# Hybrid mLSTM and Hyena backbone on one core: long filters made in the first mixer's output projection; their spectra, the addition of expert results and the row norm in one stage

## The chip, the core and the metric

The kernel runs on one core of a Trainium2 chip. TensorE (PE, with its weight loads as PEld), VectorE (DVE), ScalarE (ACT), GpSimd (POOL) and SyncE (SP, which here only issues transfers) run their own instruction streams and wait for each other by semaphores. The metric is the device time of one execution in microseconds; lower is better.

## What is computed

Two trunk layers over 512 latent tokens of width 1024, with 256 context tokens: an mLSTM mixer, then a Hyena mixer, each followed by a routed expert FFN (32 experts, top 2 in one of 4 groups). All in float32. The part that matters here:

```python
def hyena_filters(L, w1, b1, freq, w2, b2, w3, decay):
    ...
    z = jnp.sin(fr * (feat @ w1.astype(f32) + b1.astype(f32)))
    z = jnp.sin(fr * (z @ w2.astype(f32) + b2.astype(f32)))
    z = z @ w3.astype(f32)
    filt = z * jnp.exp(-tau[:, None] * decay.astype(f32)[None, :])
    return filt * lax.rsqrt(jnp.sum(filt * filt, axis=0, keepdims=True) + EPS)

def fft_long_conv(u, filt, bias):
    ...
    spec = jnp.fft.rfft(uf, n=n, axis=1) * jnp.fft.rfft(filt, n=n, axis=0)[None]
    y = jnp.fft.irfft(spec, n=n, axis=1)[:, L // 2:L // 2 + L]

# reference(), per layer i:
        ul = to_scan_order(rmsnorm(hl, norm1_g[i]) * (1.0 + sc1) + sh1, col_major)
        # layer 0: yl = mlstm_mixer(ul, ...)    layer 1: yl = hyena_mixer(ul, ...)
        hl = hl + g1 * from_scan_order(yl, col_major)
        vl = rmsnorm(hl, norm2_g[i]) * (1.0 + sc2) + sh2
        hl = hl + g2 * moe_ffn(vl.reshape(-1, D), *mo).reshape(B, S, D)
    return rmsnorm(hl, final_g)
```

The filters (512 positions by 2 x 1024 columns) depend on weights alone, not on the tokens. Each column is divided by its norm, and the kernel adds the filter's bias at the centre position.

## The kernel before

The program is a row of stages. Each is a block in which every engine has its own list of instructions in written order; a stage ends with a barrier of all engines and the clearing of its semaphores (`retire`). Nothing of a stage starts before the stage ahead has ended, so order inside a stage is set by the code, and overlap between stages does not exist. The residual stream `hl` (128 partitions x 4 row tiles x 1024) stays on chip.

1. Modulation and input projection (to about 300 us of the trace).
2. The mLSTM heads (block at L1596 to L1942, to 741 us). For each of 4 heads TensorE projects 2 q results, 4 k results (two 512 and two 256 columns wide) and 6 v results (`project`), multiplies the values of the head before (`values`), forms 6 score results, transposes the head before back (`back`) and sums denominators. Results of the projections and scores go round four PSUM banks; `begin(n)` waits until result n - 4 has been copied out (`freed`). ScalarE copies v (L1696), scales the conv output (L1692, which from head 2 on waits for `s_y`, VectorE's gating of two heads before), copies the numerators (L1684) and takes exponentials (L1703). VectorE copies q (L1783) and k (L1788), and then normalises, multiplies scores, finishes the head before, takes reciprocals (L1812) and scales `PW`.
3. Output projection (L1944): TensorE runs over 4 heads, 4 row tiles and 2 column halves with 4 accumulating matmuls each into 8 banks (L1963; each f32 matmul is 2 instructions in the trace, so 128 are 256). `residual` (L186, L187) adds the banks times the gate to `hl` after the last head. SP loads the weights of heads 1 to 3.
4. Routing and experts of layer 0 (`expert_ffn`), then `combine`: SP loads the sorted-back results (`yg`, four transfers of 1 MB), VectorE adds two weighted rows per token (L229).
5. `filters` (L740 to L886): 13 small loads; the two sine layers of the small network on 64 partitions (L787, L789, L850 to L855, L818); 16 filter tiles of 128 positions x 512 columns (L797), each multiplied by its envelope (L823, L861), squared on ScalarE (L834) and summed over positions by matmuls that give one column of 128 (L782) per quarter. The norms so lie as 128 x 16 numbers; `rsqrt` (L99 to L104: 2 integer operations and 12 float ones, each waiting for the one before) inverts them, four matmuls spread them over partitions (L804), VectorE scales the tiles (L873 to L876). Then 6 spectra (L732, L735; 3 groups of frequencies for each of 2 filters): TensorE fills four banks, ScalarE copies two of them (L839, L840), VectorE writes 4 sums and differences to `Fs` (L883 to L886). The spectra alternate between banks 0 to 3 and 4 to 7.
6. `hyena_mix` (L902): squares of the rows on ScalarE (L959), `rsqrt`, scaled rows `xh` (L999), transposes (L1078) with ScalarE writing `uh` (L963), then the projections (L1156), convolutions, forward and inverse transforms, output.
7. Routing, experts and `combine` of layer 1, and a last stage with the final row norm (L2006 to L2017) and the stores.

## Time and profile before

| | us |
|---|---|
| runs | 2569.49, 2572.08, 2572.23 (median 2572.08) |
| the profiled execution | 2573.89, span 2572.2, mean granted TensorE clock 0.906 |
| busy in the span | TensorE 2143.8, VectorE 804.0, ScalarE 275.0, GpSimd 286.7 |
| heads of the mLSTM, from 360 to 741 | 381 |
| output projection, from 741 to 856 | 115 |
| routing of layer 0, from 856 to 922 | 66 |
| experts of layer 0, from 922 to 1456 | 534 |
| adding the results, from 1456 to 1473 | 17 |
| filters and spectra, from 1473 to 1612 | 139 |
| row norm to the first projection, from 1612 to 1631 | 19 |
| last two stages, from 2539 | 33 |

The profile takes one execution; times in it are microseconds from the span's start. A timeline row gives the start, the length, the engine, the line in the kernel, the output tile and its inputs, how many instructions are merged in the row, and in brackets how long the engine had been idle and what released it. Rows of one engine overlap a little, since the next instruction starts while the last one drains. PEclk is the share of full clock granted to TensorE: 1.0 is 2.4 GHz, 0.5 is 1.2 GHz.

### The profile page before, as it was taken

How to read it: one execution, taken by the hardware profiler on the slowest of the kernel's cores; microseconds unless marked ns; L12 is line 12 of the kernel's file. 1: busy time of each engine (PE TensorE's matmuls, PEld its weight loads, DVE VectorE, ACT ScalarE, POOL GpSimd, SP SyncE). 2: the span in 40 equal slices, each digit the busy share in tenths (PEclk: the TensorE clock that was granted, in tenths of full speed). 3: DMA queues.
4: the chain of work that ended last, by engine and by line, in shares of the span. 5: the costliest groups of instructions: out<-in, count | busy, mean ns of one | idle time of the engine just before them, and what ended most of it. 6: DMA issues, size and time to landing. Idle time of an engine off the chain costs nothing. (4 is left out here: it accounts for less than half of the span.)

```text
span 2572.2 us, 20183 instructions
## 1 busy us (share of the span) xinstructions
PE 2143.8 (83%) x7640; PEld 978.2 (38%) x7640; DVE 804.0 (31%) x1407; ACT 275.0 (11%) x503; POOL 286.7 (11%) x545
## 2 busy tenths in 40 slices
PE   5998999999789669888887489799996698888972
PEld 2554444444334423333333143344454233333320
DVE  3775204325520531111111224255745311111113
ACT  2111212201100100000000031211101000000000
POOL 0000000000000312121221000000003121212210
PEclk9999999999889679999999758899996799999996
DMA  8897412220020669999999320112017699999992
GB/s 325 325 362 253 160 50 98 92 88 17 0 98 0 261 243 407 407 407 408 407 404 407 150 66 1 62 63 69 17 66 273 233 407 407 407 408 407 405 377 112
DMA packets 179008, 588.31 MB, mean 229 GB/s; under 512 B 22408, under 2 KB 40064, under 8 KB 171529
## 3 DMA queue, kind: packets, MB, share of 16 engines
q1 hardware_dynamic: 153470, 548.51, 54.9%
q10 hardware_dynamic: 13260, 21.40, 2.4%
q0 software_dynamic: 12160, 16.83, 1.9%
q8 instruction: 75, 1.23, 0.2%
q14 instruction: 43, 0.35, 0.0%
HBM read 571.61 MB, written 38.12 MB: 237 GB/s over the span
## 5 line engine op out<-in xcount | busy, mean ns | idle before, releaser
L603 PE MATMUL bank<-w,xT0e 128*64 128x512 f32 x1184 | 283.0, 633 | 59.2 <-DMA w<-in_moe_w 57.9
L603 PE MATMUL bank<-w,xT1e 128*64 128x512 f32 x1152 | 278.0, 638 | 58.6 <-DMA w<-in_moe_w 57.3
L603 PEld LDWEIGHTS bank<-w,xT0e 128*64 128x64 f32 x1184 | 104.5, 146 | 233.4 <-issue 231.5
L603 PEld LDWEIGHTS bank<-w,xT1e 128*64 128x64 f32 x1152 | 101.6, 147 | 230.9 <-issue 228.9
L1156 PE MATMUL bank<-uhi,wnh 128*128 128x512 f32 x384 | 168.4, 593 | 0.9 <-ACT uhi L963 0.9
L623 PE MATMUL bank<-w,hT0e 128*64 128x512 f32 x592 | 135.2, 597 | 8.3 <-issue 7.3
L623 PE MATMUL bank<-w,hT1e 128*64 128x512 f32 x576 | 131.5, 597 | 7.7 <-issue 6.6
L1505 PE MATMUL bank<-uT,wo 128*128 128x512 f32 x256 | 132.0, 597 | 0.5 <-DVE uT L1393 0.5
L691 DVE COPY hT0e<-bank 128x256 f32<-128x256 f32 x37 | 15.7, 425 | 311.4 <-PE bank L611 311.4
L691 DVE COPY hT1e<-bank 128x256 f32<-128x256 f32 x36 | 15.3, 425 | 312.1 <-PE bank L611 312.1
L1842 PE MATMUL bank<-uT,wo 128*128 128x512 f32 x256 | 110.7, 593 | 0.0
L1156 PEld LDWEIGHTS bank<-uhi,wnh 128*128 128x128 f32 x384 | 71.8, 190 | 86.9 <-issue 85.8
L1416 DVE SCALAR_TENSOR_TENSOR acc<-adab,cv,acc 128x2048 f32<-128x2048 f32 x35 | 82.3, 2350 | 16.9 <-DMA adab<-in_ada_w 16.1
L1654 POOL TENSOR_SCALAR_AFFINE_SELECT PW<-PW 128x128 f32<-128x128 f32 x32 | 10.9, 344 | 654.4 <-ACT PW L1703 653.1
L1893 PE MATMUL bank<-vw,xmh 128*128 128x512 f32 x192 | 83.0, 592 | 0.0
L1963 PE MATMUL bank<-ow,yT 128*128 128x512 f32 x192 | 82.6, 592 | 0.0
L1506 PE MATMUL bank<-uT,wo 128*128 128x256 f32 x256 | 76.1, 379 | 0.0
L623 PEld LDWEIGHTS bank<-w,hT0e 128*64 128x64 f32 x592 | 46.7, 136 | 73.0 <-issue 73.0
L623 PEld LDWEIGHTS bank<-w,hT1e 128*64 128x64 f32 x576 | 45.5, 136 | 70.6 <-issue 70.6
L1506 PEld LDWEIGHTS bank<-uT,wo 128*128 128x128 f32 x256 | 48.6, 190 | 61.2 <-issue 61.2
L1842 PEld LDWEIGHTS bank<-uT,wo 128*128 128x128 f32 x256 | 48.4, 190 | 61.6 <-issue 61.6
L696 DVE TENSOR_TENSOR yb0e<-bank,g2h 128x512 f32<-128x512 f32 x37 | 25.6, 692 | 122.4 <-PE bank L623 115.8
(580 smaller groups left out, 2544.9 us busy)
## 6 DMA issues: line engine op xcount, KB each, us to landing
w<-in_moe_w SPq DMA_DIRECT2D x65, 4096.0 KB, 29.1
w<-in_moe_w SPq DMA_DIRECT2D x65, 2048.0 KB, 23.9
adab<-in_ada_w SPq DMA_DIRECT2D x24, 2048.0 KB, 11.4
wnh<-in_h_in_w SPq DMA_DIRECT2D x12, 1024.0 KB, 5.2
wo<-in_m_in_w SPq DMA_DIRECT2D x4, 2048.0 KB, 10.8
wo<-in_m_in_w ACTq DMA_DIRECT2D x4, 2048.0 KB, 17.2
yg<-d_y SPq DMA_DIRECT2D x8, 1024.0 KB, 6.9
d_xm<-xmb ACTq DMA_DIRECT2D x16, 385.5 KB, 5.9
```

The lines of the kernel that those rows point to most:

```text
L603: ins = t_.matmul(b[n * C:(n + 1) * C, :].rearrange("c (g f) -> c g f", g=2), xT[:, k, half * C:(half + 1) * C], w13s[:, u, kk, n], start= ...
L623: ins = t_.matmul(b_y[m * C:(m + 1) * C, :], hT[:, k, half * C:(half + 1) * C], w2[:, u, kk, m * 512:(m + 1) * 512], start=(kk == 0), stop ...
L691: v.tensor_copy(hT[:].rearrange("p k n -> p (k n)"), b_h[:, 0:2 * P]).then_inc(S["hT"], 1)
L696: v.tensor_tensor(yb[:], b_y[:], g2h[:], ALU.mult).then_inc(S["ya"], 1)
L1156: ins = t_.matmul(bank[i % 2][:], wn[:, q % 2, k, f * P:(f + 1) * P], uh[:, k, :], start=(k == 0), stop=(k == KD - 1))
L1416: ins = v.scalar_tensor_tensor(out=a_, in0=w, scalar=s, in1=a_, op0=ALU.mult, op1=ALU.add)
L1505: t_.matmul(bank[2 * (i % 2)][:], w, uT[:, k, CTX:NTOK], start=(k == 0), stop=(k == KD - 1))
L1506: ins = t_.matmul(bank[2 * (i % 2) + 1][:, 0:CTX], w, uT[:, k, 0:CTX], start=(k == 0), stop=(k == KD - 1))
L1654: g.affine_select(out=dg, in_=dg, compare_op=ALU.is_ge, fill=0.0, base=0, pattern=[[step, P]], channel_multiplier=-step).then_inc(s_msk, 1)
L1842: ins = t_.matmul(bank[n % 4][:], wo[h % 2][:, k, f * P:(f + 1) * P], uT[:, k, CTX:NTOK], start=(k == 0), stop=(k == KD - 1))
L1893: ins = t_.matmul(b, xmh[:, f, c0:c0 + P], vw[:, f, :], start=(f == 0), stop=(f == FT - 1))
L1963: ins = nc.tensor.matmul(bank[2 * t + n][:], yT[:, i * FT + f, t * P:(t + 1) * P], ow[i][:, f, n * 512:(n + 1) * 512], start=(i == 0 and f ...
```

## The change

Four things change.

First, in the heads, the six copies of q and k per head go from VectorE's list to ScalarE's, between the scaling of the conv output and the copies of v.

Second, `filters` disappears as a stage. What makes the filters moves into the stage of the output projection. The projection is split into column halves: half 0 over all heads into banks 0 to 3, then half 1 into the same banks. Banks 4 and 5 take filter tiles, 6 and 7 the column sums. From the sixth group of half 0 on, one tile and one column sum follow each group; the last five tiles follow behind half 0. The sums are now formed with a full matrix of ones over 512 columns, so each partition holds them, and `rsqrt` works on 128 x 512 elements, four times. Finished filters are stored to memory (`d_fl`, 4 x 1 MB).

Third, `hyena_mix` loads the filters back, and in one stage forms the six spectra, adds the expert results (`combine` is gone as a stage) and takes the row norm. The filters and results use tiles that are free at that time.

Fourth, the last stage adds the expert results of layer 1, with the squares of a row tile following its addition.

```diff
-        def combine(l, wts):
-            with stage() as c:
...
+        def load_results(sp, l, yg, s_yg):
+            for t in range(TL):
+                sp.dma_start(yg[t], d_y[l].rearrange("(t p k) d -> t p k d", p=P, k=2)[t]).then_inc(s_yg[t], 16)
+
+        def add_results(dve, own, t, yg, s_yg):
+            dve.wait_ge(s_yg[t], 16)
+            for k in range(2):
+                own(nc.vector.scalar_tensor_tensor(out=hl[:, t, :], in0=yg[t][:, k, :], scalar=wts[:, k, t:t + 1], in1=hl[:, t, :], op0=ALU.mult, op1=ALU.add))
...
-        def filters(Fs, wn, s_wn):
...
@@ hyena_mix, SP
+                    sp.dma_start(dft[:], I["dft"].rearrange("(t p) f -> p t f", p=P)).then_inc(S["dft"], 16)
+                    for o in range(2):
+                        for h in range(2):
+                            sp.dma_start(flo[o][:, :, h * 512:(h + 1) * 512], d_fl[2 * o + h]).then_inc(s_flo[o], 16)
+                        if o == 0:
+                            load_results(sp, 0, yg, s_yg)
+                    for q in range(2):
+                        load_slab(sp, wn, s_wn, q)
@@ hyena_mix, ScalarE
+                    for i in range(6):
+                        odd_parts(i)
+                        if i in (1, 2):
+                            for t in range(2 * i - 2, 2 * i):
+                                act.wait_ge(S["hl"], t + 1)
+                                at_least(act, S["sq"], t)
+                                a.activation(junk, hl[:, t, :], ACT.Square, accum_out=ss[:, t:t + 1]).then_inc(S["sq"], 1)
@@ hyena_mix, VectorE
+                    for i in range(6):
+                        filter_spectra(i)
+                        if i < 2:
+                            for t in range(2 * i, 2 * i + 2):
+                                add_results(dve, own, t, yg, s_yg)
+                                v.memset(r1[:, t:t + 1], 0.0).then_inc(S["hl"], 1)
+                        if i == 3:
+                            dve.wait_ge(S["sq"], TL)
...
+                            rsqrt(v, own, r1[:], ss[:], r2[:])
+                            for t in range(TL):
+                                v.tensor_scalar(xh[:, t, :], hl[:, t, :], ss[:, t:t + 1], None, ALU.mult).then_inc(S["xh"], 1)
@@ hyena_mix, TensorE
+                    pe.wait_ge(S["dft"], 16)
+                    for i in range(6):
+                        o, g = i // 3, i % 3
+                        if g == 0:
+                            pe.wait_ge(s_flo[o], 32)
+                        at_least(pe, S["fs"], i - 1)
+                        spectrum(t_, dft, lambda pk, h: flo[o][:, pk, h * 512:(h + 1) * 512], lo if i % 2 == 0 else hi, g).then_inc(S["sps"], 1)
                     pe.wait_ge(S["xh"], TL)
+                    pe.wait_ge(S["fs"], 5)
@@ output projection, SP (after ten small loads of the filters)
                 for i in range(1, HEADS):
                     sp.dma_start(ow[i], out_rows(i)).then_inc(s_ow[i], 16)
+                for n in range(4):
+                    sp.wait_ge(s_fin, n + 1)
+                    sp.dma_start(d_fl[n], fl[n // 2][:, :, (n % 2) * 512:(n % 2 + 1) * 512]).then_inc(s_flst, 16)
+                sp.wait_ge(s_flst, 64)
@@ output projection, VectorE
+                for i in range(NT4):
+                    dve.wait_ge(s_zps, 3 + i)
+                    dve.wait_ge(s_E, i + 1)
+                    v.tensor_tensor(tile(i), bank[4 + i % 2][:], E[:, i % 2, :], ALU.mult).then_inc(s_g, 1)
+                    if i % TL == 1 and i > TL:
+                        square_sum(i // TL - 1)
                 dve.wait_ge(s_x4, 32)
+                add_projection(0)
+                square_sum(3)
+                for n in range(4):
+                    dve.wait_ge(s_smv, n + 1)
+                    r = fsum[:, n, :]
+                    rsqrt(v, own, kx[:], r, ft[:])
...
+                    own(v.tensor_tensor(centre, centre, r, ALU.mult))
+                    v.tensor_tensor(centre[0:1, :], centre[0:1, :], brow[:, cs], ALU.add)
+                    for t in (0, 2, 3):
+                        x = tile(n * TL + t)
+                        ins = v.tensor_tensor(x, x, r, ALU.mult)
+                    ins.then_inc(s_fin, 1)
+                add_projection(1)
@@ output projection, TensorE (FIRST = 5)
+                pe.wait_ge(s_fld, 16 * 6)
+                t_.matmul(bank[4][0:HFH, :], fw1[:], ft[0:HEMB, :], start=True, stop=True).then_inc(s_zps, 1)
+                for g, (i, t) in enumerate(groups):
+                    project(0, i, t)
+                    if g == 2:
+                        pe.wait_ge(s_zz, 1)
+                        t_.matmul(bank[4][0:HFH, :], fw2[:], z[0][:], start=True, stop=True).then_inc(s_zps, 1)
+                    if g >= FIRST:
+                        filter_tile(g - FIRST)
+                    if g >= FIRST + 1:
+                        square_column(g - FIRST - 1)
+                done = len(groups) - FIRST
+                for i in range(done, NT4):
+                    filter_tile(i)
+                    square_column(i - 1)
+                square_column(NT4 - 1)
+                for i, t in groups:
+                    project(1, i, t)
@@ last stage, VectorE
+                for t in range(TL):
+                    add_results(dve, own, t, yg, s_yg)
+                    v.memset(r1[:, t:t + 1], 0.0).then_inc(s_hlf, 1)
```

The functions named in it do this: `add_projection(n)` takes the four banks of a half, each a product with the gate and an addition to `hl`; `square_sum(n)` copies a sum out of its bank with the epsilon added; `filter_tile` and `square_column` are one matmul each, the first waiting for VectorE's multiplication two tiles back, the second for ScalarE's square of its tile; `odd_parts` and `filter_spectra` are the copies and sums that `filters` had.

The order of the instructions shows it at three places. VectorE, heads: behind head 0's scaling of `PW` stand, before, the copies of head 1's q and k.

```order
L1819 TENSOR_TENSOR PW<-PW,uT 128x128
L1819 TENSOR_TENSOR PW<-PW,uT 128x512
L1822 TENSOR_TENSOR PW<-PW 128x128
L1783 COPY qT<-bank 128x512 x2
L1788 TENSOR_SCALAR kT<-bank 128x512
L1788 TENSOR_SCALAR kT<-bank 128x256
L1788 TENSOR_SCALAR kT<-bank 128x512
L1788 TENSOR_SCALAR kT<-bank 128x256
L1758 BN_STATS st<-hh 128x6 x4
```

After, the statistics of head 0's values follow at once; `L1655` is the line of the statistics, `L1707` and `L1710` those of the scaling.

```order
L1707 TENSOR_TENSOR PW<-PW,uT 128x128
L1707 TENSOR_TENSOR PW<-PW,uT 128x512
L1710 TENSOR_TENSOR PW<-PW 128x128
L1655 BN_STATS st<-hh 128x6 x4
L1658 BN_AGGR mv<-st 128x2 x3
L1659 BN_AGGR mv<-st 128x2
L1660 TENSOR_SCALAR var<-mv 128x4
L99 TENSOR_SCALAR r<-var 128x4
```

The copies have left VectorE's row. On ScalarE they now stand behind the four scalings (written to a part of `wo`):

```order
L1580 ACTIVATE wo<-xch,colT 128x512 x4
L1584 ACTIVATE qT<-bank 128x512 x2
L1589 ACTIVATE kT<-bank 128x512
L1589 ACTIVATE kT<-bank 128x256
L1589 ACTIVATE kT<-bank 128x512
L1589 ACTIVATE kT<-bank 128x256
L1593 ACTIVATE wo<-bank 128x512 x6
```

There they come ahead of the six v copies. TensorE, output projection (`uT` holds the weights of head 0, `ow` the others, `fw` and `z` belong to the small network), before:

```order
L1523 UNCONDITIONAL_BRANCH
L1955 UNCONDITIONAL_BRANCH
L1963 MATMUL bank<-uT,yT 128x512 x32
L1963 MATMUL bank<-ow,yT 128x512 x96
L1944 UNCONDITIONAL_BRANCH
```

After:

```order
L1977 MATMUL bank<-ft,fw 64x512
L1955 MATMUL bank<-uT,yT 128x512 x12
L1982 MATMUL bank<-z,fw 64x512
L1955 MATMUL bank<-uT,yT 128x512 x4
L1955 MATMUL bank<-ow,yT 128x512 x8
L1966 MATMUL bank<-fw,z 128x512
L1955 MATMUL bank<-ow,yT 128x512 x4
L1966 MATMUL bank<-fw,z 128x512
L1973 MATMUL bank<-sqf,onesmat 128x512
L1955 MATMUL bank<-ow,yT 128x512 x4
L1966 MATMUL bank<-fw,z 128x512
L1973 MATMUL bank<-sqf,onesmat 128x512
```

The projection that was one run of 128 matmuls is now cut after every four by a tile and a column sum. TensorE, between the experts of layer 0 and the Hyena projections, before (the last tile, the sums, the spread norms, the spectra, and in the next stage the transposes):

```order
L797 MATMUL bank<-w3f,z1f 128x512
L782 MATMUL bank<-onesmat,sqf 128x1 x8
L804 MATMUL bank<-dgf,onesmat 128x512 x4
L732 MATMUL bank<-flf,dftf 128x512 x16
L735 MATMUL bank<-flf,dftf 64x512 x16
L732 MATMUL bank<-flf,dftf 128x512 x16
L735 MATMUL bank<-flf,dftf 64x512 x16
L740 UNCONDITIONAL_BRANCH
L1071 UNCONDITIONAL_BRANCH
L1078 MATMUL bank<-ident,Pri 128x128 x32
L1156 MATMUL bank<-uhi,wnh 128x512 x16
```

After (`vti` and `uhi` hold the filters that were loaded back):

```order
L493 UNCONDITIONAL_BRANCH
L950 UNCONDITIONAL_BRANCH
L720 MATMUL bank<-vti,dfti 128x512 x16
L723 MATMUL bank<-vti,dfti 64x512 x16
L720 MATMUL bank<-uhi,dfti 128x512 x16
L723 MATMUL bank<-uhi,dfti 64x512 x16
L965 MATMUL bank<-ident,Pri 128x128 x32
L1044 MATMUL bank<-uhi,wnh 128x512 x16
```

The spectra are now the first work behind the experts, and no barrier stands between them and the transposes.

## Rows read from the trace of the kernel before

**Rows 1.** Stages: stretch, length, busy PE PEld DVE ACT POOL, PEclk, DMA share, GB/s
```profile
741.00:856.00 115.00, 112.45 (x256) 49.50 (x256) 11.06 (x16) 0.00 (x0) 0.00 (x0) 0.98 0.14 55
1473.00:1564.00 91.00, 71.00 (x172) 39.64 (x172) 29.43 (x69) 22.55 (x35) 0.00 (x0) 0.51 0.17 51
```

**Rows 2.** TensorE's timeline, heads 0 to 3: start, us, line, work, [idle before <-releaser]
```profile
430.75 5.33 PE L1884 MATMUL bank<-xch,kw 128*128 128x512 f32 x16
441.10 7.69 PE L1884 MATMUL bank<-xch,kw 128*128 128x512 f32 x16 [5.03 <-DVE qT L1783]
...
528.52 8.35 PE L1884 MATMUL bank<-xch,kw 128*128 128x512 f32 x16 [5.03 <-DVE qT L1783]
...
557.31 20.76 PE L1903 MATMUL bank<-wo,PW 128*128 128x512 f32 x48
...
616.60 6.99 PE L1884 MATMUL bank<-xch,kw 128*128 128x512 f32 x16 [5.03 <-DVE qT L1783]
...
702.71 23.74 PE L1903 MATMUL bank<-wo,PW 128*128 128x512 f32 x48 [16.46 <-DVE PW L1822]
```

**Rows 3.** Groups by line, ScalarE in the heads: xcount | busy us, mean ns | idle
```profile
L1684 ACT ACTIVATE hh<-bank 128x512 f32<-128x512 f32 x16 | 9.6, 598 | 107.8 <-PE bank L1903 107.8
```

**Rows 4.** VectorE's timeline after head 0, ScalarE's timeline before head 2
```profile
440.36 1.28 DVE L1783 COPY qT<-bank 128x512 f32<-128x512 f32 x2
...
508.54 2.56 ACT L1692 ACTIVATE wo<-xch,colT 128x512 f32<-128x512 f32 x4 [11.83 <-DVE yT L1777]
```

**Rows 5.** Timeline of the output projection, TensorE, and the next stage's first transfer
```profile
741.35 30.05 PE L1963 MATMUL bank<-uT,yT 128*128 128x512 f32 x64 [4.48 <-PEq L121]
771.23 82.56 PE L1963 MATMUL bank<-ow,yT 128*128 128x512 f32 x192
...
856.56 0.34 SPq L259 DMA_DIRECT2D vt0r<-in_norm_g  x1
```

**Rows 6.** Timeline, start of the filter stage, all engines
```profile
1473.36 0.38 SPq L759 DMA_DIRECT2D ftf<-in_feat_t  x1
...
1478.33 1.96 PE L787 MATMUL bank<-ftf,w1f 33*64 33x512 f32 x2 [36.43 <-DMA pcf<-in_h_f_freq]
...
1481.71 0.42 DVE L852 TENSOR_SCALAR kxf<-kxf 64x512 f32<-64x512 f32 x1
...
1484.05 0.63 ACT L818 ACTIVATE z0f<-z0f 64x512 f32<-64x512 f32 x1 [46.86 <-DVE z0f L855]
```

**Rows 7.** VectorE's timeline, first block of the filter scaling
```profile
1558.89 0.68 DVE L874 TENSOR_TENSOR flf<-flf,browf 1x512 f32<-1x512 f32 x1
1559.50 1.86 DVE L876 TENSOR_TENSOR flf<-flf,bank 128x512 f32<-128x512 f32 x3
```

**Rows 8.** TensorE's timeline, two of the sixteen filter tiles
```profile
1500.77 2.07 PE L797 MATMUL bank<-w3f,z1f 64*128 64x512 f32 x2
...
1504.56 2.07 PE L797 MATMUL bank<-w3f,z1f 64*128 64x512 f32 x2
```

**Rows 9.** Timeline, expert results added and row norm; first projection of the Hyena mixer
```profile
1456.32 2.39 SPq L220 DMA_DIRECT2D yg<-d_y  x4
...
1620.40 2.74 DVE L999 TENSOR_SCALAR Pri<-hl,ssi 128x1024 f32<-128x1024 f32 x4
...
1630.95 14.00 PE L1156 MATMUL bank<-uhi,wnh 128*128 128x512 f32 x32 [0.87 <-ACT uhi L963]
```

**Rows 10.** Transfers of the expert results, both layers, by tile
```profile
DMA to landing us min/median/max: 4.7/6.9/8.8
```

**Rows 11.** TensorE's timeline, spectra 3 and 4 of six
```profile
1587.17 14.00 PE L732 MATMUL bank<-flf,dftf 128*128 128x512 f32 x32
```

**Rows 12.** Timeline of the last two stages: VectorE, ScalarE, VectorE
```profile
2543.95 10.53 DVE L229 SCALAR_TENSOR_TENSOR hl<-yg,wts,hl 128x1024 f32<-128x1024 f32 x8 [19.51 <-DMA yg<-d_y]
...
2555.83 1.06 ACT L2006 ACTIVATE junkf<-hl 128x1024 f32<-128x1024 f32 x1 [41.86 <-PEq L121]
...
2560.56 0.17 DVE L2013 TENSOR_SCALAR ssz<-ssz 128x4 f32<-128x4 f32 x1 [6.08 <-ACT junkf L2006]
```

326 lines of the change are left out of this document (136 added, 190 removed).

## The prediction

> **What bounds the kernel now.** I read the view of stages first, then TensorE's timeline through each stage that the diff touches, then, where TensorE stood idle, the timeline of the engine named behind the arrow. Four places come out.
>
> In the four heads of the first mixer TensorE runs nearly without a break, except that heads 1 to 3 each stop for 5.03 us in the middle of the k projection, until VectorE has copied the first q result out of its bank [rows 2]. VectorE does that copy at 440.36, behind the reciprocal and scaling of the head before [rows 4]. After each stop the 16 matmul instructions take 7.69, 8.35 and 6.99 us, where the 16 of the same shape ahead of the stop took 5.33 [rows 2].
>
> In the output projection TensorE is the bound: 112.45 of 115 us busy at a granted clock of 0.98, the 2.4 GHz level [rows 1, 5].
>
> From 1473 to 1564 us the filters are made by a chain of three engines. TensorE counts 71 of 91 us as busy, but its clock is 0.51, the 1.2 GHz level [rows 1], and its tiles come 3.79 us apart (1500.77 to 1504.56) [rows 8].
>
> Between the first transfer of the expert results at 1456.32 and the Hyena mixer's first projection at 1630.95 lie 174.6 us [rows 9]: adding the results, the filters, their spectra, and the row norm, one after another.
>
> **Step 1, q and k copied out by ScalarE.** Removed: 6 copies per head in VectorE's queue. Added: 6 on ScalarE, each about 0.60 us, the price of its other copies from a bank [rows 3]. In ScalarE's queue they stand behind the four scalings of the head's conv output. Before head 2 those start at 508.54, held by VectorE's gating of head 0, and end at 511.1 [rows 4]. The stop of that head begins at 528.52 - 5.03 = 523.5 [rows 2], behind two q results and two k results (3 x 3.44 us, and 1.7 for the one of 256 columns: 12.0), so the first q result starts at about 511.5 and is complete at 514.9: ScalarE is free in time, by 3.8 us. A bank is then emptied 0.6 us after it is full, and is wanted again only three results later: the stop goes. Gain 3 x 5.03 = 15.1 us, and the slow matmuls behind it, 7.69 + 8.35 + 6.99 - 3 x 5.33 = 7.0 us: **-22.1**. The later waits of a head hang on TensorE's own value products and move along with them. Bounds: -15.1, if the clock still falls for another reason, and -22.1.
>
> **Step 2, the filters in the output projection's stage.** Before, from TensorE's first matmul at 741.35 to the next stage's first transfer at 856.56, this took 115.2 us [rows 5]. I count after from the stage's start, S.
> - TensorE now waits first for six small loads. In the filter stage these cost 1478.33 - 1473.36 = 5.0 us [rows 6].
> - Up to the second half's first matmul it has half of the projection, 128 instructions, 4 of the small network, 32 of tiles and 32 of column sums: 196, at 82.56 / 192 = 0.43 us each [rows 5] 84.3 us.
> - The start at 1.2 GHz: 48 instructions took 23.74 us after a wait of 16.46, and 20.76 without [rows 2]: 3.0 us. For the last five tiles, which no projection covers, I add 1.5 us (estimate; a tile and a column sum fill 1.72 us of TensorE, and VectorE's 0.68 and ScalarE's 0.63 follow each other beside it).
> So the second half starts at S + 93.8. The small network's first sine ends 6.4 us after its matmul began (1478.33 to 1484.68) [rows 6], less than the three projection groups of 3.4 us set in front of the next one: no wait. The 6 MB of output weights are now queued behind 1.6 MB more; the first is wanted only after four groups, 23 us in, so I cost that at nothing; without that cover it would be a few us.
> - From there TensorE needs 128 x 0.43 = 55.0 us, but VectorE more. It starts about 1.6 us ahead, on four bank additions of two operations each (8 x 0.72 = 5.8) and one sum (0.7). Then come four blocks: an inverse square root over 128 x 512 elements, which was over 128 x 16. Its two integer operations at 0.45 (0.42 for a 512-wide operation with constants [rows 6], and the step to the next) and twelve at 0.72 (0.68 [rows 7] and the step) give 9.5; the scaling is 0.72 + 0.61 + 1.86 = 3.1 [rows 7]. Four blocks are 50.6 us. The filters are complete at +55.5, and four more bank additions end at +61.3. The last 1 MB store, of the size of the result loads, takes 4.7 to 6.9 us [rows 10] and lands at about +61.5. The end of a stage costs 0.7, half of the 1.35 us from 2554.48 to 2555.83, where two are closed [rows 12].
> The stage lasts 93.8 + 61.5 + 0.7 = 156 us and a little for a store that takes longer; I take 157: **+41.8**. VectorE, not TensorE, ends it. Bounds: +35 if the wide operations run at the 0.62 pitch of the scaling and TensorE ends the stage (55.0 + 1.4 for the last addition), +52 if each tile's wait costs TensorE 0.6 us more. The routing stage behind it begins with TensorE idle for 7 us instead of 3: **+1** (0 to 2).
>
> **Step 3, spectra, expert results and norm in one stage.** Instead of 174.6 us I find: 0.7 for one stage end more in front; 9.5 until the transform matrix and the first filters (2.9 MB) have landed, since four result transfers of 1 MB land 4.7 to 8.8 us after issue [rows 10] and the four together took about 11 (range 7 to 14); the first spectrum, 7.0 (half of 14.00 [rows 11]) and 3.0 for the clock; five more at 7.03, 35.2; then 7.8 from the transposes to the first projection (1623.14 to 1630.95 [rows 9]). VectorE fits under it: six spectra at 2.4 us, eight result additions at 1.32 (10.53 for eight [rows 12]), 3 us of small operations and 2.74 us of row scaling [rows 9] make 31 us, in 42. In its order, the scaled rows are ready 30.6 us after the first spectrum's end and the fifth spectrum's sums at 33, and TensorE comes to the transposes at 35.2. No bank is waited for: spectrum 4 needs the sums of spectrum 2, ready at 20, and starts at 21. The clock, now at 2.4 GHz through the transposes, may give 1 us. Sum 63.2: **-111.4**. Bounds -116 and -105.
>
> **Step 4, the last stage.** The squares of a row tile now run under the next tile's addition: 2555.83 to 2560.56 are 4.7 us, of which the last square, 1.3, stays; and 0.7 of a stage end goes: **-4.1** [rows 12].
>
> **The sum:** -22.1 + 41.8 + 1 - 111.4 - 4.1 = -94.8. The profiled execution took 2573.9 us (span 2572.2, and 1.7 around it), and would take 2479.1. The median of the runs, 2572.1, gives **2477**. The two expert stages only move in time: their weight transfers start with the routing stage, as before.
>
> **Rivals.**
> A: ScalarE comes no earlier to the q results than VectorE did, because its scalings wait for VectorE's gating. Then step 1 brings nothing: 2477 + 22 = 2499. Against it stand the 3.8 us of slack, and that the gating itself moves forward with the head.
> B: the filter tiles keep their own chain inside the projection. If each of 16 costs 3.79 us as in [rows 8] instead of 1.72, that is 16 x 2.07 = 33 us more: 2510. For it: the order of engines is the same. Against it: 11 of the 16 have four projection matmuls (3.4 us) between them, longer than VectorE's and ScalarE's shares together.
> C, the other side: the merged stage runs at 1.2 GHz. In the filter stage just these tiles and sums ran at a clock of 0.51 although TensorE was busy for 78% of it [rows 1]. TensorE would then need 5 + 196 x 0.86 + 1.5 + 128 x 0.86 = 285 us and 2 for the end, 130 more than forecast: 2607, slower than before. It decides from 95 / 0.43 = 221 of the 324 instructions at the low level. Against it: 256 of them are the same projection matmuls that ran at 0.98 [rows 1], and the waits in between are under 1 us.
> The Trainium skill speaks for C: "TensorE: Matmul & The Clock Gate", section "A second HAM failure mode: psum-queue depth-cycling", says that short idles between groups of matmuls, as banks are cycled, can make the clock swing between its levels. By that rule the time would be C's or a part of it; in the heads of this trace banks are cycled all the time, and only the 5 us stops are followed by slow matmuls [rows 2], so the trace does not agree with it for waits this short.
>
> **How the numbers follow.** Forecast 0.77, with a range of its own of 2464 to 2492 (steps 2 and 3 by their bounds, not both at their ends). A 0.10, B 0.09, C 0.04. The range reaches to A and leaves out B, C and the forecast's own ends: 2464 to 2501. A change under 0.2% can't be told from none here. Forecast, A and B are faster: 0.95; C is slower: 0.04; 0.01 for a mixture that cancels out.
>
> **What would show it.** Right: no wait of TensorE on q copies; the next stage after the projection 157 us after its start, with VectorE last; the projection at a clock above 0.95; 63 us from the end of the first expert stage to the Hyena mixer's first projection. Wrong: a falling clock in the projection, square root operations over 0.72 us, spectra that wait for filters from memory beyond 14 us, or transposes that wait for VectorE.

## The result and the profile after

The changed kernel takes 2450.07 us (median of 4 runs, 2449.15 to 2453.90), the kernel before 2570.86 beside it (4 runs, 2569.49 to 2572.23): a ratio of 0.9533, with a 95% interval of 0.9516 to 0.9550. That is faster, as forecast, but by 120.8 us instead of 95, and 2450 lies outside the range of 2464 to 2501. The profiled execution has a span of 2452.2 us, 120.0 less than that of before.

The first thing to do with such a miss is to cut both traces at the same points and subtract. SyncE's first transfer of each stage is a good mark, since nothing of a stage starts before it. These are the marks after, from SyncE's timeline (start, length, line, what is loaded):

```profile
717.38 0.32 SPq L1857 DMA_DIRECT2D ft<-in_feat_t  x1
...
879.24 0.35 SPq L247 DMA_DIRECT2D vt0r<-in_norm_g  x1
...
1470.61 0.38 SPq L777 DMA_DIRECT2D dfti<-in_dft  x1
...
1849.16 0.34 SPq L247 DMA_DIRECT2D vt1r<-in_norm_g  x1
...
2423.83 2.07 SPq L212 DMA_DIRECT2D ygf<-d_y  x4
```

The same marks before are 741.30, 856.56 [rows 5], 1456.32 [rows 9] and these two:

```profile
1947.88 0.34 SPq L259 DMA_DIRECT2D vt1r<-in_norm_g  x1
...
2539.21 1.91 SPq L220 DMA_DIRECT2D yg<-d_y  x4
```

The Hyena mixer's first projection stands at 1630.95 [rows 9] before and at 1532.14 after.

| stretch | before | after | difference | forecast |
|---|---|---|---|---|
| start to output projection | 741.3 | 717.4 | -23.9 | -22.1 (Step 1) |
| output projection stage | 115.3 | 161.9 | +46.6 | +41.8 (Step 2) |
| routing and experts of layer 0 | 599.8 | 591.4 | -8.4 | +1 (Step 2) |
| first result transfer to first projection | 174.6 | 61.5 | -113.1 | -111.4 (Step 3) |
| rest of the Hyena mixer | 316.9 | 317.0 | +0.1 | 0 |
| routing and experts of layer 1 | 591.3 | 574.7 | -16.6 | 0 |
| last stage | 33.0 | 28.4 | -4.6 | -4.1 (Step 4) |

The four steps together miss by 1 us, and that is partly luck: Step 2 came out 4.8 us dearer, and Steps 1, 3 and 4 together 4.0 us better. What the forecast missed lies in the routing and expert stages, where the diff changes no instruction's work and only moves one small tile: 25 us less, where it had said +1. TensorE there waits for weights. In the view of waits (in us: total, times, longest), TensorE's waits for the weight transfers, both layers together, stood at 115.1 us before:

```profile
PE bank L603 <- DMA w<-in_moe_w: 115.1, 38, 4.7
```

and after they are 19 us shorter:

```profile
PE bank L591 <- DMA w<-in_moe_w: 95.8, 35, 4.3
```

The windows view shows more. Of two stretches of 200 us inside the expert stages it gives the busy time of PE, PEld, DVE, ACT, POOL, then the clock, the DMA share and the GB/s. Before:

```profile
1100.00:1300.00 200.00, 166.01 (x738) 64.59 (x736) 24.92 (x56) 10.79 (x28) 40.11 (x85) 0.95 1.03 407
2130.00:2330.00 200.00, 174.30 (x774) 67.90 (x774) 24.91 (x56) 10.78 (x28) 39.53 (x85) 0.94 1.03 407
```

After:

```profile
1100.00:1300.00 200.00, 174.72 (x792) 69.33 (x790) 26.68 (x60) 11.55 (x30) 42.60 (x90) 0.96 1.03 419
2130.00:2330.00 200.00, 173.75 (x790) 68.75 (x788) 26.69 (x60) 11.55 (x30) 40.19 (x86) 0.97 1.02 419
```

The DMA engines are busy throughout in both (shares of 1.02 and 1.03), but move 419 GB/s instead of 407. So the question is not when these transfers start, but why the same transfers run 3% faster.

### The profile page after: what moved, and what is told of

Its sections match the earlier page's. It is cut to its first block and busy times, and to the rows that moved or that the text cites. A ratio compares the mean times of both kernels' runs of the same rounds, so it can differ in the third digit from the quotient of the medians.

```text
span 2452.2 us, 19965 instructions
## 1 busy us (share of the span) xinstructions
PE 2091.9 (85%) x7536; PEld 944.2 (39%) x7536; DVE 825.7 (34%) x1420; ACT 289.5 (12%) x529; POOL 286.7 (12%) x545
## 5 line engine op out<-in xcount | busy, mean ns | idle before, releaser
L591 PE MATMUL bank<-w,xT1e 128*64 128x512 f32 x1152 | 271.9, 626 | 49.8 <-DMA w<-in_moe_w 48.3
L1730 PEld LDWEIGHTS bank<-uT,wo 128*128 128x128 f32 x256 | 48.4, 190 | 61.5 <-issue 61.5
L662 ACT ACTIVATE sg0e<-bank 128x256 f32<-128x256 f32 x37 | 14.3, 385 | 452.3 <-PE bank L591 452.3
## 6 DMA issues: line engine op xcount, KB each, us to landing
w<-in_moe_w SPq DMA_DIRECT2D x65, 4096.0 KB, 28.4
```

The lines of the kernel that those rows point to most:

```text
L591: ins = t_.matmul(b[n * C:(n + 1) * C, :].rearrange("c (g f) -> c g f", g=2), xT[:, k, half * C:(half + 1) * C], w13s[:, u, kk, n], start= ...
L662: a.activation(sg[:], b_gu[u][:, 0:DE // 2], ACT.Silu).then_inc(S["sg"], 1)
L1730: ins = t_.matmul(bank[n % 4][:], wo[h % 2][:, k, f * P:(f + 1) * P], uT[:, k, CTX:NTOK], start=(k == 0), stop=(k == KD - 1))
```

## Experiments: why the expert weights arrive faster

One tile that the diff moves offers a reason.

```diff
+        wts = sbt(top, "wts", [P, 2, TL])
...
-                wts = sbt(c, f"wts{l}", [P, 2, TL])
```

The small tile `wts` (32 bytes in each partition) moves from the expert stage, where it stood behind the weight tiles, to the top of on-chip memory, and pushes all that comes behind it up by 32 bytes. Read from the addresses that the program is built with, the weight tile `w13` (two thirds of the weight bytes; rows of 4096 bytes) goes from byte 37088 of each partition to 37120, and `w2` from 135392 to 135424. The first pair are multiples of 32 only, the second of 256. The diff also declares a new tensor in main memory, `d_fl`, which moves `d_y`, where results are scattered. I tested both.

**Undoing the shift in the changed kernel.** Two pads in the expert stage alone; the rest of the change stays.

```diff
+                pa = sbt(c, f"pa{l}", [P, 8])
                 w13 = sbt(c, f"w13_{l}", [P, NB, KD, 2 * DE])
...
                 g2h = sbt(c, f"g2h{l}", [P, D // 2])
+                pb = sbt(c, f"pb{l}", [P, 8])
```

> The changed kernel, computing the same, with 32 bytes a partition put ahead of the expert weight tiles in the expert stages and 32 more behind them. The change had moved a 32-byte tile (wts) to the top of the on-chip memory, so that the weight tiles w13 and w2 start at byte 37120 of each partition, a multiple of 64, where they started at 37088, a multiple of 32 only. This kernel puts them at 37152, a multiple of 32 only, and leaves all else of the change. Theory P (place of the weight tiles): the two expert stages lose what they won, about 8 + 17 = 25 us, so 2475 us, and the transfers in them run at 406 to 408 GB/s instead of 418 to 420. Theory M (place in main memory: the new tensor d_fl moves d_y, to which results are scattered): nothing changes, 2450 us and 419 GB/s. Theory O (another part of the change, or the chip's own spread): nothing changes either.

Measured: 2477.56 us, ratio 0.9645 (0.9629 to 0.9661). Routing and experts take 602.5 and 587.8 us instead of 591.4 and 574.7, and the gain of these stages is gone. This is the changed kernel with its weight tiles at bad places, as they were before, and so the kernel that the prediction priced: 2477.6 us against the forecast 2477, a sum whose terms partly cancel. The two stretches of 200 us:

```profile
1100.00:1300.00 200.00, 172.77 (x774) 67.74 (x770) 25.36 (x58) 11.26 (x30) 39.66 (x84) 0.95 1.03 407
2130.00:2330.00 200.00, 166.74 (x732) 64.52 (x732) 24.89 (x56) 10.65 (x28) 37.05 (x79) 0.93 1.03 407
```

**The same pads in the kernel before**, with nothing else of the change.

> The kernel before, computing the same, with the same 32 bytes ahead of the expert weight tiles, which puts w13 at 37120, a multiple of 64. Theory P: 25 us faster than the kernel before, about 2547 us, with 418 to 420 GB/s in the expert stages. Theories M and O: no change, 2572 us and 407 GB/s.

Measured: 2546.26 us, ratio 0.9912 (0.9895 to 0.9928), 23 us faster (19 to 27 by the interval); the two stretches are 585.7 and 576.6 us long.

```profile
1100.00:1300.00 200.00, 169.50 (x764) 66.55 (x764) 25.98 (x59) 11.17 (x30) 39.63 (x84) 0.96 1.03 420
2130.00:2330.00 200.00, 176.45 (x794) 69.40 (x792) 25.98 (x59) 11.54 (x30) 42.08 (x88) 0.95 1.03 419
```

**The new tensor in main memory alone**, declared in the kernel before and not used.

```diff
         d_v = [dram(f"d_v{i}", [SEQ, D]) for i in range(2)]
+        d_fl = dram("d_fl", [4, P, TL, 512])
```

> The kernel before, computing the same, with the new tensor d_fl declared in main memory but not used, so that d_y0 and d_y1 lie 4 MB further, as in the changed kernel. Theory M: 25 us faster, about 2547 us, 419 GB/s in the expert stages. Theories P and O: no change, 2572 us, 407 GB/s.

Measured: 2569.84 us, ratio 1.0000 (0.9990 to 1.0009), and 407 GB/s. Theories M and O fall. The place of the tiles in the expert stage carries the 25 us: taken away in the changed kernel, it costs 27.5 us, and given to the kernel before, it brings 23.

**Which places are good.** Two runs with 64 bytes ahead of `w13`, as here, and with 128 (32 elements of 4 bytes instead of 16):

```diff
+                pa = sbt(c, f"pa{l}", [P, 16])
                 w13 = sbt(c, f"w13_{l}", [P, NB, KD, 2 * DE])
```

> The changed kernel, computing the same, with 64 bytes ahead of w13: both weight tiles start at a multiple of 64 that is no multiple of 128 (37184 and 135488), where the changed kernel's were multiples of 128. If a multiple of 64 is what counts: no change, ratio 0.9533, 419 GB/s in the expert stages. If a multiple of 128 counts: as with 32 bytes, 0.9645 and 407 GB/s, or something between.

Measured: 2478.43 us, ratio 0.9637 (0.9621 to 0.9653), 407 GB/s. I had expected a multiple of 64 to be enough. It is not.

> The changed kernel, computing the same, with 128 bytes ahead of w13: w13 at 37248 and w2 at 135552, both odd multiples of 128, where the changed kernel's 37120 and 135424 were multiples of 256. Shifts of 32 and of 64 bytes cost 24 to 28 us each. If a multiple of 128 is what counts: no change, ratio 0.9533, 419 GB/s in the expert stages. If a multiple of 256 counts: 0.964 and 407 GB/s. (37120 is no multiple of 512, so nothing beyond 256 is needed.)

Measured: 2478.16 us, ratio 0.9644 (0.9628 to 0.9660), again 407 GB/s. A multiple of 128 is not enough either. So far three shifts cost the same, and the changed kernel's place might have been good for some reason of its own. The run with 256 bytes tells:

> The changed kernel, computing the same, with 256 bytes ahead of w13: w13 at 37376 and w2 at 135680, both multiples of 256. Shifts of 32, 64 and 128 bytes cost 24 to 28 us each (ratios 0.9637 to 0.9645, 407 GB/s in the expert stages). Theory (a multiple of 256 bytes is what counts): as the changed kernel, ratio 0.953, 419 GB/s. Rival (37120 is good for another reason, such as its distance to other tiles, and any shift spoils it): 0.9640, 407 GB/s.

Measured: 2451.48 us, ratio 0.9532 (0.9517 to 0.9548), stretches of 589.3 and 575.1 us:

```profile
1100.00:1300.00 200.00, 176.14 (x796) 69.73 (x794) 26.68 (x60) 11.52 (x30) 40.71 (x87) 0.96 1.03 419
2130.00:2330.00 200.00, 173.92 (x790) 69.07 (x792) 26.68 (x60) 11.49 (x30) 41.44 (x89) 0.97 1.02 419
```

A multiple of 256 bytes is what counts among the places tried; how far off it the tile lies (32, 64, 128, or 224 as before) makes no difference that these runs can tell. The Trainium skill has a rule that fits: "DMA: Bandwidth & Descriptors", section "How a descriptor splits into AXI transactions", says that the transactions of a transfer start at 256-byte boundaries, so that a piece which doesn't begin at one has its first transaction start at the boundary below, and spends beats of 32 bytes on what lies before its start. That page of the Trainium skill speaks of reading, while the tiles here are written to. As an estimate from the same page of the Trainium skill, if a row of 4096 bytes is one piece of 128 beats, 32 bytes off would add 1 beat (0.8%), 128 bytes 4 (3.1%) and 224 bytes 7 (5.5%). The runs agree with the boundary, but not with a cost by beats: here all of these places cost 2.9% (407 against 419). Why the price is the same at every distance stays open.

**Which tile.** Four runs misplace one tile alone, or both by different amounts. The pad in front of `w2` moves the small tiles behind it too. First `w2` by 32 bytes:

> The changed kernel, computing the same, with 32 bytes between w13 and w2: w13 stays at a multiple of 64 and only w2, a third of the bytes, goes to a multiple of 32 only. Theory P with a cost per byte: a third of the 25 us comes back, 8 us, so 2458 us, with 415 GB/s in the expert stages; the median time to landing of the w2 transfers (24.0 us) grows and not that of w13 alone. If only the first tile's place counted, 2450 us; if any misplaced tile spoiled the whole, 2475 us. Theories M and O: 2450 us.

Measured: 2455.89 us, ratio 0.9560 (0.9544 to 0.9576), 418 GB/s, stretches of 592.4 and 576.9 us. The median time to landing of the `w2` transfers did not grow: 23.4 us, and 24.0 in the changed kernel. Then by 64 bytes:

> The changed kernel, computing the same, with 64 bytes between w13 (stays at 37120) and w2 (135488, an odd multiple of 64). With 32 bytes there the ratio was 0.956, 3 to 7 us over the changed kernel; with 32 ahead of w13 and 64 ahead of w2 it was 0.9634, and with 64 ahead of both 0.9637. If the cost lies with the w13 transfers mostly: a ratio of 0.954 to 0.957 again and 418 GB/s. If it is a cost per byte of whichever tile: 0.957, 415 GB/s. If one misplaced tile of two were enough for the whole at this distance: 0.9635, 407 GB/s.

Measured: 2453.56 us, ratio 0.9545 (0.9529 to 0.9561), 419 and 417 GB/s, stretches of 590.8 and 576.2 us. Then 32 bytes ahead of `w13` and 32 behind it:

> The changed kernel, computing the same, with 32 bytes ahead of w13 and 32 behind it: w13, two thirds of the weight bytes, starts at a multiple of 32 only, w2 at a multiple of 64. Putting both there cost 25 us (ratio to the kernel before 0.9645 instead of 0.9533), w2 alone 3 to 7 us. Theory P with a cost per byte: two thirds of 25 us, 17 us, a ratio of 0.960. Theory P with w13 as the carrier (w2 alone cost less than its third): 18 to 22 us, 0.9605 to 0.962. Had the cost lain only in both being misplaced together: under 5 us, 0.955.

Measured: 2478.38 us, ratio 0.9634 (0.9618 to 0.9650). I had planned it as a run with `w13` alone misplaced, and counted a multiple of 64 as a good place for `w2`. The runs above show that it is none, so this run has both misplaced and says only that the two offsets need not be equal. The run that does separate them:

```diff
+                pa = sbt(c, f"pa{l}", [P, 32])
                 w13 = sbt(c, f"w13_{l}", [P, NB, KD, 2 * DE])
+                pb = sbt(c, f"pb{l}", [P, 32])
```

> The changed kernel, computing the same, with 128 bytes ahead of w13 and 128 behind: w13 at an odd multiple of 128 (37248), w2 at a multiple of 256 (135680). w2 alone misplaced gave ratios of 0.956 and 0.9545 against 0.9533. Theory (w13 carries it): 0.9625 to 0.9645. A cost per byte: 0.960. If both have to be misplaced: 0.953 to 0.955.

Measured: 2464.49 us, ratio 0.9584 (0.9568 to 0.9600), and between the two rates:

```profile
1100.00:1300.00 200.00, 174.67 (x786) 68.61 (x783) 25.99 (x59) 11.54 (x30) 39.77 (x84) 0.95 1.03 414
2130.00:2330.00 200.00, 174.69 (x780) 68.00 (x779) 24.91 (x56) 10.77 (x28) 40.05 (x85) 0.94 1.02 414
```

So `w13` alone costs about 13 us and both together 24 to 29. That meets none of the three expectations for this last run; the nearest is the cost per byte, 0.960, at the edge of the interval. What `w2` alone costs is less sure. By the ratios its two runs lie 3 and 7 us above the changed kernel, but the intervals overlap with that kernel's. The two expert stages together took 1167.0 and 1169.2 us in them, and 1164.4 to 1168.9 in the seven runs made from the changed kernel with both tiles well placed, where single stretches of 200 us show 417 to 420 GB/s. Both tiles misplaced cost more than the two costs added; a transfer into a well placed tile seems to take up part of what a misplaced neighbour in the queue loses. That is a reading, and no run isolates it.

**Is it general?** The big early loads go to places that are no multiples of 256 in both kernels.

```diff
+        pc = sbt(c12, "pc12", [P, 32])
         wo = [sbt(c12, f"wo{i}", [P, KD, DH]) for i in range(2)]
...
+            pd = sbt(c1, "pd", [P, 48])
             adab = [sbt(c1, f"adab{i}", [P, 2, 2048]) for i in range(2)]
```

> The changed kernel, computing the same, with the targets of the big early loads put at multiples of 256 bytes: adab0 and adab1 (from 173504 and 189888 to 173824 and 190208) and wo0 and wo1 (from 94592 and 110976 to 94720 and 111104). Up to 200 us of the trace these loads keep the DMA engines busy nearly throughout (shares of 0.97, 0.77, 1.00 and 0.96 in four stretches of 50 us) but TensorE too. If the rule is general and the early stages hang on the loads: 3 per cent of up to 150 us, 4 to 5 us less, ratio 0.9515. If TensorE's work hides the loads, or if the rule holds for the expert weights alone: no change, 0.9533.

Measured: 2452.15 us, ratio 0.9534 (0.9518 to 0.9550): no change that can be told. The `adab` transfers did land a little earlier. By tile, their time to landing in the changed kernel (minimum, median, maximum) is

```profile
DMA to landing us min/median/max: 7.8/11.3/19.7
```

and in this run

```profile
DMA to landing us min/median/max: 7.6/10.9/19.2
```

The output projection begins at 715.48 here, and between 716.43 and 719.00 in the other runs made from the changed kernel, so up to 1 us may have been won. The place is worth something where a stage hangs on its transfers, as the expert stages do; here TensorE is busy beside them.

## Experiments: the steps of the prediction

**Step 1 alone.** The six copies of q and k move to ScalarE in the kernel before.

```diff
-                if kind == "v":
+                if kind in ("q", "k", "v"):
...
+                    for i in range(QT):
+                        n = NUM["q", h, i]
+                        act.wait_ge(s_pj, n + 1)
+                        a.activation(qT[:, i, :], bank[n % 4][:], ACT.Copy).then_inc(s_evA, 1)
```

> The kernel before, computing the same, with the first part of the change alone: the six copies of q and k of each head by ScalarE. The prediction's Step 1: 22.1 us faster, ratio 0.9914, and TensorE waits for no copy of q in the second to fourth head, head period 80 us. Rival A (ScalarE comes late from head 2 on): 0 to 11 us, ratio over 0.9957. If the first part only helped together with the others, no change, ratio 1.0.

Measured: 2546.69 us, ratio 0.9900 (0.9884 to 0.9917), 25 us faster. TensorE's timeline shows the k projection in one piece, where before it was two with a stop between them [rows 2]:

```profile
429.92 10.49 PE L1884 MATMUL bank<-xch,kw 128*128 128x512 f32 x32
...
509.76 10.49 PE L1884 MATMUL bank<-xch,kw 128*128 128x512 f32 x32
...
589.61 10.49 PE L1884 MATMUL bank<-xch,kw 128*128 128x512 f32 x32
```

Each head now takes 79.8 us.

**Step 2, its start.** TensorE's first projection group goes ahead of its wait for the filter loads.

```diff
-                pe.wait_ge(s_fld, 16 * 6)
-                t_.matmul(bank[4][0:HFH, :], fw1[:], ft[0:HEMB, :], start=True, stop=True).then_inc(s_zps, 1)
                 for g, (i, t) in enumerate(groups):
                     project(0, i, t)
-                    if g == 2:
+                    if g == 0:
+                        pe.wait_ge(s_fld, 16 * 6)
+                        t_.matmul(bank[4][0:HFH, :], fw1[:], ft[0:HEMB, :], start=True, stop=True).then_inc(s_zps, 1)
+                    if g == 3:
```

> The changed kernel, computing the same, with TensorE's list at the start of the output projection in another order: the first group of the projection stands ahead of the small network's first matmul and its wait for the filter loads, and the second matmul one group later. In the changed kernel TensorE stands idle there for 5.0 us, and its clock is at half until 5.6 us later. Theory: the idle time goes, 5 us less, 2445 us, ratio 0.9513, and the second half of the projection starts 94 to 95 us after the stage's start instead of 99.8. Rival: the wait for the copy of z moves behind and gives it back, or the half clock holds as long after the first matmul as now (then about 7 us of the first groups' work still runs at half): 2 to 3 us less. If the end of the stage hung on VectorE's chain from a fixed time, no change.

Measured: 2445.66 us, ratio 0.9509 (0.9493 to 0.9525). The stage takes 156.6 us (718.53 to 875.12) and its second half starts at 813.08, 94.6 us after its start. The wait is gone and nothing took its place.

**Step 2, its layout.** GpSimd adds the squares of a block, 4 column sums replace 16, filter tiles run on into the second half, and VectorE inverts blocks between tiles.

```diff
+            @blk.gpsimd
...
+                        own(nc.gpsimd.tensor_tensor(fsum[:, n % 3, :], fsum[:, n % 3, :], sqf[:, t % 2, :], ALU.add))
...
+                AFTER = {5: [(inverse, 0)], 7: [(scaled, 0)], 10: [(add_projection, 0)], 11: [(inverse, 1)], 13: [(scaled, 1)],
+                         14: [(inverse, 2)], 15: [(scaled, 2), (inverse, 3), (scaled, 3)]}
...
+                    if j in (4, 8, 12, 19):
+                        column_sum(min(j // TL - 1, 3))
```

> The changed kernel, computing the same, with the output projection's stage laid out anew: TensorE starts at once (as in the run before), filter tiles go on one per group into the second half, GpSimd adds the squares of a block so that 4 column sums on TensorE take the place of 16, and VectorE inverts and scales the blocks between the tiles. Theory (the stage is bound by TensorE's list up to the second half and then by VectorE's chain of 62 us, so what counts is TensorE's work and an earlier start of that chain): TensorE's 256 projection instructions at 0.43 us, 110 us, plus 16 tiles and 4 sums at 0.96, 19, plus 5 us for the network and the slow clock, plus 3 us at the end: 137 us for the stage instead of 161.9, so 25 us less, 2425 us, ratio 0.9436. Rival (VectorE falls behind, so that TensorE waits for banks while a block is inverted, or GpSimd's additions slow VectorE): 10 to 18 us less, 0.9465 to 0.9495. Rival (the stage is bound by the VectorE chain however it starts): no more than the 5 us of the run before, 0.9510.

Measured: 2441.80 us, ratio 0.9499 (0.9483 to 0.9514): the stage takes 149.7 us instead of 161.9, not 137. TensorE's timeline names two waits:

```profile
785.66 2.08 PE L1990 MATMUL bank<-fsum,onesmat 128*128 128x512 f32 x2 [4.44 <-POOL fsum L1907]
787.52 4.29 PE L1974 MATMUL bank<-ow,yT 128*128 128x512 f32 x8
...
798.93 5.40 PE L1974 MATMUL bank<-uT,yT 128*128 128x512 f32 x8 [1.38 <-DVE tmp L1927]
```

After each wait its instructions are slower: 5.40 us for 8, where 3.70 is the rule in this stage. The first wait is for GpSimd, and GpSimd's timeline shows an operation of one size at two prices:

```profile
749.05 1.27 POOL L1907 TENSOR_TENSOR fsum<-fsum,sqf 128x512 f32<-128x512 f32 x1 [101.16 <-ACT sqf L1896]
753.80 1.27 POOL L1907 TENSOR_TENSOR fsum<-fsum,sqf 128x512 f32<-128x512 f32 x1 [3.47 <-ACT sqf L1896]
...
780.61 5.00 POOL L1907 TENSOR_TENSOR fsum<-fsum,sqf 128x512 f32<-128x512 f32 x2 [10.53 <-ACT sqf L1896]
...
820.01 2.92 POOL L1907 TENSOR_TENSOR fsum<-fsum,sqf 128x512 f32<-128x512 f32 x1 [11.67 <-ACT sqf L1896]
...
835.12 3.44 POOL L1907 TENSOR_TENSOR fsum<-fsum,sqf 128x512 f32<-128x512 f32 x1 [10.54 <-ACT sqf L1896]
```

An addition took 1.27 us while VectorE was idle, and 2.92 and 3.44 beside VectorE's scaling, which reads two on-chip tiles. GpSimd's spans are rough, but VectorE's own operations beside it went up too, as this one of the scaling, which takes 0.68 otherwise [rows 7]:

```profile
781.03 1.64 DVE L1946 TENSOR_TENSOR wo<-wo,brow 1x512 f32<-1x512 f32 x1
```

**The same, with two orders changed**, so that a sum is asked for later and the bank additions stand ahead of a tile.

```diff
-                AFTER = {5: [(inverse, 0)], 7: [(scaled, 0)], 10: [(add_projection, 0)], 11: [(inverse, 1)], 13: [(scaled, 1)],
+                AFTER = {5: [(inverse, 0)], 7: [(scaled, 0)], 9: [(add_projection, 0)], 11: [(inverse, 1)], 13: [(scaled, 1)],
...
-                    if j in (4, 8, 12, 19):
-                        column_sum(min(j // TL - 1, 3))
+                    if j in (4, 10, 13, 19):
+                        column_sum((4, 10, 13, 19).index(j))
```

> The kernel of the run with the projection stage laid out anew (0.9499), computing the same, with two waits of TensorE taken out by order alone: the second and third column sum stand two groups and one group later, and VectorE adds the first half of the projection ahead of the eleventh filter tile instead of behind it. In that run TensorE waited 4.44 us for a slow addition on GpSimd and 1.38 us for a bank, and ran some 3 us slower behind them. Theory: 5.8 us of waits and about 3 us of slow clock go, 2433 us, ratio 0.9465. Rival (the sums wait at their new places, since GpSimd's additions take 3 to 5 us beside VectorE's): 2 to 4 us, 0.9485.

Measured: 2434.77 us, ratio 0.9467 (0.9452 to 0.9483). The stage takes 140.5 us, and between its first matmul and the next stage TensorE waits for no other engine. This kernel beats the changed one by 0.6% to 0.7%, with intervals that do not overlap, and is the fastest of the study. The gain of 7 us is for both orders together.

**Step 3, the overlap alone.** Results and norm come behind all six spectra, still in one stage.

```diff
                     for i in range(6):
                         filter_spectra(i)
-                        if i < 2:
-                            for t in range(2 * i, 2 * i + 2):
-                                add_results(dve, own, t, yg, s_yg)
...
+                    for t in range(TL):
+                        add_results(dve, own, t, yg, s_yg)
+                        v.memset(r1[:, t:t + 1], 0.0).then_inc(S["hl"], 1)
```

> The changed kernel, computing the same, with the results added and the row norm taken after all six spectra instead of between them, still in one stage. It tells what of Step 3 is overlap. In the changed kernel the transposes start at 1524.97 with no wait for VectorE. Here VectorE's eight additions (1.3 us each), the last square, the inverse root and the four scalings (10.5 + 1.3 + 3.1 + 2.7 us) come behind its last writes of the spectra (3.7 us after the last spectrum): 21 us later, 2471 us, ratio 0.9615. With TensorE's clock at half after the idle time, the transposes take some 3 us more, 2474 us, 0.9627. If the overlap were worth little because the transfers of the results end late, under 10 us.

Measured: 2475.73 us, ratio 0.9630 (0.9614 to 0.9646). By the trace the stretch to the first projection grows from 61.5 to 82.5 us (1471.41 to 1553.95), and TensorE waits where the changed kernel does not:

```profile
1517.79 7.09 PE L723 MATMUL bank<-uhi,dfti 128*64 128x512 f32 x32
1546.15 5.41 PE L962 MATMUL bank<-ident,Pri 128*128 128x128 f32 x24 [21.28 <-DVE Pri L875]
```

So 21 of the 113 us of Step 3 are overlap of the norm and the results. The rest is, by subtraction, the filters, which are no longer made here, and the stage ends.

## Why the prediction was wrong

**The step that failed** is the sentence behind the sum: "The two expert stages only move in time: their weight transfers start with the routing stage, as before." Their start did not change, but their rate did, from 407 to 419 GB/s, since the diff moved their target by 32 bytes onto a multiple of 256. That is 25 us by the two stretches, and 23 to 28 by the runs that move the tiles alone, of the 27 us between forecast and result. The profile of before could not show it as a gain waiting to be had: it shows one rate. What it did show is that these two stretches of some 600 us hang on the weights (115.1 us of TensorE's waits in them), so everything that touches the weight tiles, their place too, had to be looked at. The line that moves `wts` stood in the diff, and I passed over it as one without a cost. With -25 in its place the forecast would have been about 2452.

**Step 1** was right in mechanism and a little small: 23.9 us in the trace, 25 as a change of its own (interval 21 to 30), against 22.1. Of the part not counted, 0.8 us is the last head's numerator, 22.96 us for the instructions that took 23.74 [rows 2], and 0.5 us lies ahead of the second head; 0.5 us more is not traced. Rival A fell: no stop is left.

```profile
430.26 10.49 PE L1772 MATMUL bank<-xch,kw 128*128 128x512 f32 x32
...
510.11 10.49 PE L1772 MATMUL bank<-xch,kw 128*128 128x512 f32 x32
```

**Step 2** had its structure right and one term too small. The second half began 99.8 us after the stage's start, not 93.8:

```profile
722.34 1.96 PE L1977 MATMUL bank<-ft,fw 33*64 33x512 f32 x2 [9.39 <-DMA pc<-in_h_f_freq]
724.23 12.51 PE L1955 MATMUL bank<-uT,yT 128*128 128x512 f32 x24
736.67 1.07 PE L1982 MATMUL bank<-z,fw 64*64 64x512 f32 x2
...
753.91 1.13 PE L1973 MATMUL bank<-sqf,onesmat 128*128 128x512 f32 x2
754.87 3.60 PE L1955 MATMUL bank<-ow,yT 128*128 128x512 f32 x8
758.40 1.12 PE L1966 MATMUL bank<-fw,z 64*128 64x512 f32 x2
759.45 1.12 PE L1973 MATMUL bank<-sqf,onesmat 128*128 128x512 f32 x2
...
813.27 1.12 PE L1966 MATMUL bank<-fw,z 64*128 64x512 f32 x2
814.32 1.12 PE L1973 MATMUL bank<-sqf,onesmat 128*128 128x512 f32 x2
816.23 1.12 PE L1973 MATMUL bank<-sqf,onesmat 128*128 128x512 f32 x2 [0.78 <-ACT sqf L1891]
817.19 8.32 PE L1955 MATMUL bank<-uT,yT 128*128 128x512 f32 x19
```

The start is as forecast: 5.0 us of waiting, then 14.3 us for 26 instructions, 3.1 more than at 0.43 each. The waits are small, one of 0.78 us. The term that was mis-sized is "at 82.56 / 192 = 0.43 us each" for tiles and sums. That pitch is of a row of equal matmuls. Here a tile takes 1.05 us from its start to the next (758.40 to 759.45), a sum 0.96 (759.45 to 760.41), 2.01 for a pair instead of 1.72, and in the tail, with nothing else between, a pair takes 2.11 (1.05 and 1.06). Sixteen pairs make 5 us of the 6. That the change of shape is the price, and not the sum itself, shows in the run with the new layout: there a sum takes 0.86 us (838.74 to 839.60) between projection groups of its own shape, and 0.96 (809.99 to 810.95) behind a tile. This is a term mis-sized inside its bounds (+35 to +52). From there the forecast held: the stage ended 62.05 us after the second half began (61.5 and 0.7 forecast), with VectorE last. Its four blocks came every 12.76 us; the first root's two integer operations, priced at 0.42 and the step to the next, took

```profile
821.45 0.42 DVE L99 TENSOR_SCALAR kx<-fsum 128x512 int32<-128x512 int32 x1
821.90 0.43 DVE L100 TENSOR_SCALAR kx<-kx 128x512 int32<-128x512 int32 x1
```

Rival B fell by TensorE's rows: a tile and its sum cost 2.01 us between projections and 2.11 without, not 3.79 [rows 8]. Rival C fell: TensorE's granted clock in the projection stage, in a stretch of each half, is 1.00, the upper level, 2.4 GHz:

```profile
730.00:800.00 70.00, 70.00 (x154) 27.11 (x153) 11.53 (x18) 14.96 (x24) 0.00 (x0) 1.00 0.19 76
817.00:870.00 53.00, 53.00 (x125) 23.39 (x124) 50.78 (x79) 0.00 (x0) 0.00 (x0) 1.00 0.16 60
```

**Step 3** was right, 113.1 against 111.4. The first spectrum began 9.7 us after the stage's first transfer (9.5 forecast), and the six ran without a wait:

```profile
1480.31 16.77 PE L720 MATMUL bank<-vti,dfti 128*128 128x512 f32 x32 [25.96 <-DMA vti<-d_fl]
1497.00 7.09 PE L723 MATMUL bank<-vti,dfti 128*64 128x512 f32 x32
1504.02 14.00 PE L720 MATMUL bank<-uhi,dfti 128*128 128x512 f32 x32
1517.95 7.09 PE L723 MATMUL bank<-uhi,dfti 128*64 128x512 f32 x32
1524.97 1.09 PE L965 MATMUL bank<-ident,Pri 128*128 128x128 f32 x8
...
1532.14 3.27 PE L1044 MATMUL bank<-uhi,wnh 128*128 128x512 f32 x7 [0.87 <-ACT uhi L823]
```

The first one cost 2.8 us for the low clock (16.77 for a row of 32 that otherwise takes 14.00; 3.0 forecast). VectorE finished the scaled rows at 1520.4, 4.6 us ahead of the transposes; the run without overlap shows what that order is worth.

**Step 4** was right, 4.6 against 4.1, and so was the +1 for the routing, as far as it can be read: from the stage's first transfer to the first expert matmul it took 72.8 us before and 73.4 after. Two parts were also made alone in the kernel before: the copies gave 24.9 us and the place of the tiles 23; what is left of 120.8, 73 us, is the forecast of Steps 2 to 4 (41.8 + 1 - 111.4 - 4.1 = -72.7), again with Step 2's miss made up by the others.

**What stays open.** With the same places of the weight tiles, layer 0's routing and experts take 585.7 us in the kernel before with pads and 591.4 in the changed one; 0.7 of these 5.7 us lie ahead of the first expert matmul, the rest behind it. With both tiles misplaced the difference is smaller: 598.9 to 599.8 us in three kernels with the filters in their old stage, 601.2 to 602.5 in four made from the changed one. No run looked for the cause.

## What to carry to other kernels

Where a stage waits for large transfers, treat the byte at which their on-chip tile starts as part of the kernel: try a multiple of 256, which won 23 to 28 us here, and look at a diff for every tile that is added, moved or removed ahead of it, however small. When a prediction goes by parts, cut both traces at the same marks and subtract before explaining anything: here four of seven stretches agreed to 2 us, one missed by 5, and the 25 us lay in the two that nobody had changed. Price a matmul that stands between others of a different shape by its distance to the next in such a place, not by the pitch of a long equal row. And when a sum comes out right, look at its terms: here one that was 4.8 us too small hid behind three that were 4.0 us too cautious.

## What the runs showed of the hardware

In the expert stages, where the DMA engines carry 4096-byte rows of weights from memory to on-chip tiles, they moved 407 to 408 GB/s when the tiles began 32, 64, 128 or 224 bytes past a multiple of 256, and 417 to 420 when they began at one. With only the larger tile misplaced it was 414; with only the smaller one 417 to 419, which the rate alone can't tell from none. The cost was the same at each distance tried, and both tiles misplaced cost more (24 to 29 us) than one and the other added (13, and 7 at most).

GpSimd's addition of two 128x512 float32 tiles took 1.27 us alone, and 2.9 to 3.4 beside VectorE's scaling, which reads two on-chip tiles; one of VectorE's own operations went from 0.68 to 1.64 beside it. The Trainium skill, "SBUF — State Buffer", section "Who interferes with whom", names a pair of ports that the two engines share, which one instruction holds until it ends; the trace agrees that both slow down. Moving the additions of squares to GpSimd won its full price here only when no wait of TensorE for GpSimd was the next one due: the stage took 149.7 us with such a wait, and 140.5 with the two orders changed.
